# Normed rows stored in the order of the experts' weight rows, the gate matrix inside the first expert unit, and the second unit's features ahead of it

## The reference

```python
def hier_moe(h, wg, bg, we, be, w_gate, w_up, w_down):
    p_group = softmax(x32 @ wg + bg);  pg, g_sel = top_k(p_group, 1)
    e_in = (x32 @ we + be).reshape(t, 4, 8)[g_sel]
    top_v, top_i = top_k(e_in, 2)
    gates = softmax(top_v) * pg
    ids = (g_sel * 8 + top_i).reshape(-1)
    order = argsort(ids);  tok = order // 2
    xs = xf[tok]                                   # 512 rows, sorted by expert
    hg = ragged_dot(xs, w_gate, sizes)             # 1024 -> 512
    hu = ragged_dot(xs, w_up, sizes)
    ys = ragged_dot(silu(hg) * hu, w_down, sizes)  # 512 -> 1024
    ys = ys * gates.reshape(-1)[order][:, None]
    return segment_sum(ys, tok, num_segments=t)

# second_block
h2 = rmsnorm_2(x, norm2_w)
x = x + hier_moe(h2, ...)
return rmsnorm_2(x, norm_f_w)
```

## Time and profile before

| | |
|---|---|
| median of three runs | 1124.17 us (1121.33 to 1125.53) |
| profiled execution | 1122.43 us |
| its span, first to last instruction | 1120.6 us |
| PE busy | 1053.4 us, 94% of the span |
| DVE busy | 840.5 us, 75% |
| ACT busy | 660.6 us, 59% |
| mean granted TensorE clock | 0.979 |

### The profile page before, as it was taken

The page is one execution under the profiler, slowest core; times in us unless marked ns, Lnnn a source line. Parts: engine busy times, 40 slices in busy tenths (PEclk is TensorE's granted clock), DMA queues, the critical chain, the costliest instruction groups (busy, mean ns, idle before and its releaser), DMA issues.

```text
span 1120.6 us, 15061 instructions
## 1 busy us (share of the span) xinstructions
PE 1053.4 (94%) x5674; PEld 894.4 (80%) x5674; DVE 840.5 (75%) x1072; ACT 660.6 (59%) x791; POOL 34.3 (3%) x40
## 2 busy tenths in 40 slices
PE   5999999999999899898987989999999999999984
PEld 5878999999999777798877868778778787787763
DVE  4755776666677556777657679999999999999964
ACT  4554655554456644455424567777777777777742
POOL 0000000000010100100020000000000000000000
PEclk9999999999999989999999989999999999999987
DMA  9633356556424533333203659899899899899940
GB/s 337 234 113 132 117 185 225 173 166 225 156 75 159 180 114 118 110 117 113 75 31 150 225 184 391 354 355 388 351 378 366 351 383 359 355 379 364 369 154 39
DMA packets 82565, 253.60 MB, mean 226 GB/s; under 512 B 4144, under 2 KB 42160, under 8 KB 62512
## 3 DMA queue, kind: packets, MB, share of 16 engines
q1 hardware_dynamic: 81664, 251.27, 60.3%
q10 hardware_dynamic: 816, 1.23, 0.3%
HBM read 251.44 MB, written 1.05 MB: 225 GB/s over the span
## 4 chain that ended last, share of the span: by engine, by line
PE 76%; DVE 10%; ACT 7%; issue 4%; POOL 1%; DMA 1%; DVEq 0%; POOLq 0%; SPq 0%; ACTq 0%
PE bank L1698 21%; PE bank L1700 21%; PE bank L1699 21%; PE bank L2165 4%; ACT WH L484 4%; DVE WL L915 3%; PE bank L2117 1%; DVE CV L1150 1%; PE bank L2147 1%; POOL sm L1658 1%; DMA cn<-in_cn 1%; PE bank L1724 1%; ACT HTH L503 1%; PE bank L2227 1%; ACT CV L491 1%
## 5 line engine op out<-in xcount | busy, mean ns | idle before, releaser
L915 DVE TENSOR_TENSOR WL<-raw,WH 128x2048 fp32r<-128x2048 f32 (+1 forms) x235 | 503.9, 2175 | 113.3 <-ACT WH L484 113.3
L484 ACT ACTIVATE WH<-raw 128x2048 fp32r<-128x2048 f32 (+1 forms) x235 | 427.1, 1824 | 105.3 <-PE bank L1700 94.0
L1698 PE MATMUL bank<-WH,MXH 128*128 128x512 f32 x552 | 220.3, 399 | 4.1 <-DVE MXL L1591 2.7
L1700 PE MATMUL bank<-WH,MXL 128*128 128x512 f32 x552 | 216.5, 392 | 0.0
L1699 PE MATMUL bank<-WL,MXH 128*128 128x512 f32 x552 | 216.2, 392 | 0.0
L1698 PE MATMUL bank<-HTH,WH 128*128 128x256 f32 x576 | 165.8, 288 | 3.5 <-DVE CV L1150 2.6
L1699 PE MATMUL bank<-HTL,WH 128*128 128x256 f32 x576 | 163.7, 284 | 0.0
L1700 PE MATMUL bank<-HTH,WL 128*128 128x256 f32 x576 | 163.6, 284 | 0.0
L1698 PE MATMUL bank<-WH,HTH 128*128 128x512 f32 x348 | 140.4, 403 | 7.4 <-DVE BIG L1574 4.2
L1699 PE MATMUL bank<-WL,HTH 128*128 128x512 f32 x348 | 137.6, 395 | 0.0
L1698 PEld LDWEIGHTS bank<-WH,MXH 128*128 128x128 f32 x552 | 104.9, 190 | 25.4 <-DVE MXL L1591 2.8
(11 more groups left out here) (342 smaller groups left out, 1114.1 us busy)
## 6 DMA issues: line engine op xcount, KB each, us to landing
raw<-in_exp_w_gate SPq DMA_DIRECT2D x52, 1024.0 KB, 8.0
raw<-in_exp_w_up SPq DMA_DIRECT2D x52, 1024.0 KB, 7.8
raw<-in_exp_w_down SPq DMA_DIRECT2D x52, 1024.0 KB, 5.6
raw<-in_w_in SPq DMA_DIRECT2D x34, 1024.0 KB, 5.3
raw<-in_w_up SPq DMA_DIRECT2D x22, 1024.0 KB, 5.2
raw<-in_w_down SPq DMA_DIRECT2D x11, 1024.0 KB, 5.3
raw<-in_w_out SPq DMA_DIRECT2D x8, 1024.0 KB, 5.1
raw<-in_w_o SPq DMA_DIRECT2D x4, 1024.0 KB, 5.3
```

Source lines behind the costliest of these rows:

```text
L484: e.activation(WH[i % HL][:, 0:n], raw[i % RAW][:, 0:n], ACT.Copy).then_inc(a_wh, 1)
L915: e.tensor_tensor(l, r, h.bitcast(F32), ALU.subtract).then_inc(v_wl, 1)
L1698: e.matmul(out_, ah, bh, start=start, stop=False)
L1700: return e.matmul(out_, al, bh, start=False, stop=stop)
```

## The change

Four things change.

1. `H2H` and `H2L` are written in another order of columns: `in_rows`/`by_row` read every eighth number of `X` (a step of 32 bytes) and write without gaps. The stationary operand of the gathering is then 128 neighbouring columns.
2. PE builds the gate matrix between the two gate pieces and the two up pieces of unit 0. DVE computes the gates ahead of splitting the pieces NP+2 and NP+3, and not behind them.
3. ACT and DVE write the features of unit 1 earlier: ACT ahead of splitting piece NP+3, DVE ahead of `gate_hidden(0)`. DVE reads one number of the table, not three, between the masked gate matrix and unit 0's gate column; the others come later, behind the split of a piece. For unit 0's output the tile is fixed as 0.
4. The turned selection is made by a function of its own behind unit 0, in the banks 7, 5 and 6. ACT copies it out behind the splits of both NP+4 and NP+5. `turn_hidden(0)` no longer waits for that copy; `down(0)` does.

```diff
-                m = e.activation(H2H[:, t, :], X[:, t, :], ACT.Copy, scale=rs[:, t:t + 1])
+                m = e.activation(in_rows(H2H[:, t, :]), by_row(X[:, t, :]), ACT.Copy, scale=rs[:, t:t + 1])
...
+        def by_row(v):
+            return v.rearrange("q (p k) -> q k p", k=8)
+        def in_rows(v):
+            return v.rearrange("q (k p) -> q k p", k=8)
...
             load_tile(1)
+            e.wait_ge(v_xst, 4)
+            e.wait_ge(a_xst, 12)
+            features(1)
             split(NP + 3)
             e.wait_ge(p_used, NP + 2)
             e.activation(SG[0], bank[GU[0][0]][:, :], ACT.Silu).then_inc(a_sg, 1)
             split(NP + 4)
+            split(NP + 5)
             for j in range(3):
...
-                             bank[(7, 4, 5)[j]][:, 0:128 * n], ACT.Copy).then_inc(a_selT, 1)
-            split(NP + 5)
+                             bank[SELB[j]][:, 0:128 * n], ACT.Copy).then_inc(a_selT, 1)
...
-                m = e.scalar_tensor_tensor(out=H2L[:, t, :], in0=X[:, t, :], scalar=rs[:, t:t + 1],
-                                           in1=H2H[:, t, :].bitcast(F32), op0=ALU.mult, op1=ALU.subtract)
+                m = e.scalar_tensor_tensor(out=in_rows(H2L[:, t, :]), in0=by_row(X[:, t, :]), scalar=rs[:, t:t + 1],
+                                           in1=in_rows(H2H[:, t, :].bitcast(F32)), op0=ALU.mult, op1=ALU.subtract)
...
             gathered(7)
-            split(NP + 2)
-            split(NP + 3)
             e.wait_ge(a_route, A_ROUTE["dm"])
...
             e.tensor_tensor(oh1, oh1, oh2, ALU.add).then_inc(v_route, 1)
-            split(NP + 4)
+            split(NP + 2)
+            split(NP + 3)
             og, ig = (bc(v.unsqueeze(1), P, NT, 32) for v in (off, inc))
...
-            load_tile(0)
-            gate_column(0)
-            gate_hidden(0)
-            split(NP + 5)
-            load_tile(1)
+            load_code(0)
+            gate_column(0)
+            split(NP + 4)
+            load_tile(1)
+            features_low(1)
+            gate_hidden(0)
+            split(NP + 5)
+            tile[0] = 0
+            load_code(1)
+            count = e.value_load(TBI[0:1, 3:4], min_val=0, max_val=UNITS)
...
-                            m = e.matmul(bank[GATB[k]][:, 0:NS // 2], part[:, t, k:D:8], SEL[:, t, hs],
+                            m = e.matmul(bank[GATB[k]][:, 0:NS // 2], part[:, t, k * 128:(k + 1) * 128], SEL[:, t, hs],
...
                     elif u == 0:
+                        gate_matrix()
                         e.wait_ge(a_xst, 10)
...
             unit(0)
-            gate_matrix()
+            turn_selection()
```

More of the change, by code:

```diff
@@ L833, in load_tile, with features @@
                 tile[u] = e.value_load(TBI[u:u + 1, 1:2], min_val=0, max_val=NT - 1)
+            def features(u):
+                for i in range(2):
+                    xs4 = XST[i].rearrange("p k (t c) -> p k t c", t=NT)
+                    e.activation(XCH[u % 2][:, 4 * i:4 * i + 4, :].unsqueeze(2), xs4[:, :, bass.ds(tile[u], 1), :],
+                                 ACT.Copy).then_inc(a_xch, 1)
             load_tile(1)
+            e.wait_ge(v_xst, 4)
+            e.wait_ge(a_xst, 12)
+            features(1)
             split(NP + 3)
@@ L858, in unit @@
                     e.wait_ge(p_used, unit_base(u - 2) + 4)
-                else:
-                    e.wait_ge(v_xst, 4)
-                    e.wait_ge(a_xst, 12)
-                for i in range(2):
-                    xs4 = XST[i].rearrange("p k (t c) -> p k t c", t=NT)
-                    e.activation(XCH[u % 2][:, 4 * i:4 * i + 4, :].unsqueeze(2), xs4[:, :, bass.ds(tile[u], 1), :],
-                                 ACT.Copy).then_inc(a_xch, 1)
+                    features(u)
                 i = unit_base(u)
@@ L2143, in turn_hidden @@
                     e.wait_ge(v_hil, u)
-                else:
-                    e.wait_ge(a_selT, 3)
                 for k in range(4):
```

33 lines of the change are left out of this document (19 added, 14 removed).

## The result

The changed kernel takes 1111.28 us in the median of four runs (1109.4 to 1115.55); the kernel before, run beside it, 1122.99 us (four runs). The ratio is 0.9899, with a 95% interval of 0.986 to 0.9938: faster by 7.0 us at the least reading and by 15.7 at the most. The prediction was 1114.8 us, with a range of 1110.5 to 1119.5 and a chance of 0.85 for faster. The execution that was profiled is the slowest of the four, 1115.55 us (the prediction had 1113.0 for it); its span is 1113.8 us, where before had 1120.6.

What follows compares the result with a forecast made beforehand. PE, busy for 94% of the span, was taken to pace the units. Gains of 9.7 us (unit 1's start) and 2.0 (clock), less 2.3 (step), make 9.4: 1124.17 to 1114.8 us, range 1110.5 to 1119.5.

Steps and rivals of the forecast that it cites:

- The spacing: Gathering matmuls at full clock: 0.147 us each, not 0.240, with a stationary operand without a step; 4.7 us on PE.
- The step on DVE: H2L, ahead of the router's chain: reading X with a 32-byte step taken as twofold, 2.3 us lost.
- room of 3.4 us: H2H on ACT: what reading with the step may add there, as DVE takes H2H up later.
- The first rival: H2L: the step costs DVE nothing and it stays at 2.47 us; time 1112.5 us, chance 0.25.
- the slower one: H2L: the step costs DVE the whole gain, from 11.7 us on; 1129 us with the eightfold bound, chance 0.04.
- The gathering's clock: Start of the gathering: 14 matmuls at half clock gain nothing, the other 50 gain 4.7 us on PE.
- DVE's chain: DVE's work from L1501 (620.8) to the end of gate_hidden(0) (638.7) sets unit 1's start; gain 9.7 us.
- margin of 1.3 us: Gate matrix inside unit 0: PE wants the gates at 628.9, DVE has them at 627.6.
- Unit 1: Start of unit 1: its first matmul near 642, where before it was at 649.34.
- The clock: Start of unit 1: PE's clock stays full with at most 2.2 us idle; gain 2.0 us, bounds 0 and 2.0.
- the rival of the transfers: Units behind the start are paced by transfers, so the gain is lost there; 1123 to 1124 us, chance 0.08.

Runs made afterwards that it cites:

- a3: Changed kernel with H2H and H2L made from X without the 32-byte step, so features reach the experts in wrong order; 1109.26 us, ratio 0.9887.
- a5: Kernel before, with PE's two idle stretches around unit 0 filled to size by 13 and 9 idle matmuls; 1122.11 us, ratio 0.9992.
- b1: Changed kernel with only the gate matrix put back behind unit 0; 1119.45 us, ratio 0.9959.
- b2: Changed kernel with only DVE's order put back: gate_hidden(0), splits NP+4 and NP+5, then unit 1's low features; 1120.89 us, ratio 0.9979.
- b3: Changed kernel with H2L made by POOL in two steps, not by DVE; 1113.43 us, ratio 0.9918.
- c1: Changed kernel with half of each of the two gate pieces not transferred from unit 4 on; 1110.86 us, ratio 0.9900.
- c2: Kernel before with half of each of the two gate pieces not transferred from unit 4 on; 1122.88 us, ratio 0.9999.
- b4: Changed kernel with 56 instead of 36 filling matmuls ahead of the gathering; 1111.16 us, ratio 0.9879.
- a1: Kernel before with only the new row order of H2H and H2L and contiguous stationary for the gathering; 1122.74 us, ratio 0.9996.

## Why the prediction was right

**The spacing.** 0.147 us, from the straight line between two rows, is what the trace has. That 320 columns weren't what cost 0.240 was right, and so was the load as its cause: 188 ns and not 338. That the steps at half clock gain nothing was right too: 0.267 us in both kernels.

**The step on DVE.** I charged 2.3 us (twofold). H2L went from 2.47 to 4.06, 1.6 times, so 1.6 us; the rest of the 2.4 that a3 gave is a longer wait of PE ahead of the gathering and its clock, which the sum didn't have. So the term comes out right as a whole, by luck: a third too large for DVE, with nothing for PE. ACT's 1.9-fold stayed in its room of 3.4 us. The first rival (the step is free) fell, and the slower one with it: it needed 11.7 us.

**The gathering's clock.** The step of the sum here was "the 14 matmuls at half clock have no gain", and it took them as 14. They were 18, for PE had waited 4.9 us ahead of them; before, and in a3, it had waited 3.3. It costs unit 0 some 0.5 us and DVE's chain as much; the milder H2L gives that back. Unit 0 started at 625.75, where 625.7 was expected, because these two nearly cancel: that it comes to 0.1 us is luck.

**DVE's chain.** I had 17.9 us from L1501 (620.8 to 638.7) and expected it 2.3 later: 623.1 to 641.0. Measured, 623.00 to 640.59, so 17.6 us. Gates, masks and table were in time; PE came to the gate matrix at 631.22, and the gates were done at 629.6, so the margin of 1.3 us was 1.6. The one thing that waited was the one named, gate_hidden(0), for 0.44 us of PE.

**Unit 1.** Expected near 642 (641.9), measured 641.14. The 0.76 are 0.1 from the start of the chain, 0.3 from its length, and 0.35 from the transposes: the next matmul starts 0.55 us behind gate_hidden and not 0.9, for they were counted at 0.75 and overlap what follows.

**The clock.** Expected to stay, with 2.0 us to gain: it stayed, and a5 measured 1.9 for it alone. In b1 and b2, with waits of 4.6 and 4.9 us, it fell (granted 0.58 in 643.00 to 648.08 and 0.74 in 638.20 to 643.76); with 0.44 it didn't. So the gain of 2.0 us hangs on the others, and neither half of the order gets it alone.

**What was off in the sum.** 9.4 us were expected at the 12th matmul of unit 1, 10.2 measured (10.3 counted from H2H). The own time of the profiled execution was expected at 1113.0 and was 1115.55, for there the rival of the transfers held in part: it gave back 4.1 us. I had priced it as all or nothing, with a chance of 0.08, on 0.8 us of waits in the kernel before (1.3 with the down weights). A start 10 us earlier may take away some of the lead that the loads have on PE, but no run shows it: a3, with the earliest unit 1, had a rest of 427.06, and b3, at 48.13, one of 427.20 and no wait for transfers at all. Why one execution has late transfers and the next has none stays open. In the medians nothing of this is seen (c1).

The median came out 3.5 us under the forecast of 1114.8. Of this, 1.2 are the kernel before itself, 1122.99 beside the changed kernel and 1124.17 in the forecast's base; 0.9 are the sum; the other 1.4 are not explained and lie within the scatter. The difference of the medians, 11.7 us, agrees with 10.3 within its interval.

## What to carry to other kernels

When two engines wait for each other in turn around one place, look for work of the waiting one that needs nothing of the other and put it there; b1 and b2 show that half of such a reordering wins little, since the chain then only waits elsewhere. A step in an operand is paid by whoever reads or writes it, so move it from where it is used 64 times at the cost of PE to where it is used twice, and look first what stands behind those two. Compare variants by places in the trace, counted from a common event just ahead of the change: with the same code up to there, unit 1 came at 46.35 and 46.20 (changed kernel and c1) and at 54.72 and 54.68 (before and c2), where medians of 6 to 12 runs told 2 us apart. And look for what the step hides as well as for what it costs: the first 1.37 us of a faster gathering were worth their time, the rest met other work of ACT and DVE (b4).

## What the hardware showed that was not expected

A step of 32 bytes in the f32 input costs DVE 1.64 times (2.47 to 4.06 us for 2 x 1024 numbers), ACT 1.94 times (2.17 to 4.20), and PE's load 1.80 times (188 to 338 ns) at full clock, but next to nothing at half clock (330 to 338 ns): the load with the step took 338 ns at either clock. A step of 512 bytes in the output costs ACT about the same as the 32 bytes in the input (3.94). The rule of the Trainium skill (Advanced Engine Details and Errata, SBUF Cachelines), two accesses to a line or a penalty, holds in direction in all four; it gives no price, and the rows have it between 1.6 and 1.9 times.

Two of DVE's operations with two inputs were each held for a whole operation of POOL with two inputs, 2.8 us; beside POOL's operations with one input, others of DVE kept their 0.17 to 0.23 us (b3).

The transfers of the units run at 359 to 362 GB/s with the DMA engines 90% busy. One execution lost 4.1 us in them, with 17.1 us of waits of ACT for transfers, and all others between nothing and 1.8 (the column "rest"). The engines can do more: 416 GB/s, wholly busy, in b4 from 610.00 to 615.02.

The stretch ahead of the change, the same code in all these kernels, ended anywhere in 6.8 us in their profiled executions. That is more than half of the gain measured here, and may be why a1's 2.3 us and a5's 1.9 don't show in the medians.
